# Half of the experts' second product turned round: weights stationary in 64-column tiles, the other half still streaming

## The reference, cut to what matters

```python
xe = xf[idx]                                                       # 16 x 80 x 1024
he = silu(einsum('ecd,edf->ecf', xe, w1)) * einsum('ecd,edf->ecf', xe, w3)
ye = einsum('ecf,efd->ecd', he, w2) * gate[..., None]              # w2: 1024 x 1024 for each expert
y = zeros_like(xf).at[idx.reshape(-1)].add(ye.reshape(-1, dm))
```

## Time and profile before

| | |
|---|---|
| time, median of 3 executions | 3217.52 us (3211.68 to 3217.69) |
| profiled execution | 3212.84 us, span 3211.0 us |
| TensorE clock granted, mean | 0.915 of full speed |
| PE busy | 2661.8 us (83%) |
| PEld busy | 1809.8 us (56%) |
| DVE, ACT, POOL busy | 1150.1, 464.4, 755.2 us |
| bytes moved by DMA | 552.70 MB |
| the two experts' stages | 1053 to 1601 us, 2633 to 3178 us |

### The profile page before, as it was taken

How to read it: one execution, slowest core, us unless ns; L and a number is a source line. 1 busy time by engine, 2 the same in 40 slices (tenths; PEclk the granted TensorE clock), 3 DMA queues, 4 the chain that set the end, 5 groups by cost and what they waited for, 6 DMA issues and landing times. The chain is left out here.

```text
span 3211.0 us, 72150 instructions
## 1 busy us (share of the span) xinstructions
PE 2661.8 (83%) x32434; PEld 1809.8 (56%) x32434; DVE 1150.1 (36%) x2476; ACT 464.4 (14%) x957; POOL 755.2 (24%) x886
## 2 busy tenths in 40 slices
PE   6998874778784899999879978566786849999995
PEld 3564554628643666766435645355385347676672
DVE  1002668775534111111130046786845241111112
ACT  1002331042111000000020033302311010000001
POOL 0002808435212000000010046272432220000002
PEclk9998996889986999999989999877998969999997
DMA  6101000050043899999731010001400549999994
GB/s 268 59 0 39 1 10 3 1 216 5 28 198 132 319 390 398 397 393 400 269 152 46 0 39 1 10 3 47 172 30 3 209 173 379 394 390 396 400 374 140
DMA packets 73210, 552.70 MB, mean 172 GB/s; under 512 B 13848, under 2 KB 15704, under 8 KB 33992
## 3 DMA queue, kind: packets, MB, share of 16 engines
q1 hardware_dynamic: 66760, 527.11, 41.3%
q0 software_dynamic: 6144, 20.98, 2.8%
HBM read 523.54 MB, written 24.51 MB: 171 GB/s over the span
## 5 line engine op out<-in xcount | busy, mean ns | idle before, releaser
L2352 PEld LDWEIGHTS ps<-arena 128*64 128x64 f32 x16384 | 579.8, 138 | 87.3 <-issue 84.7
L2352 PE MATMUL ps<-arena 128*64 128x80 f32 x16384 | 600.2, 234 | 11.7 <-issue 7.1
L2366 PE MATMUL ps<-arena 128*80 128x512 f32 x1024 | 466.7, 600 | 0.0
L517 PE MATMUL ps<-arena 128*128 128x128 f32 (+1 forms) x1088 | 296.4, 435 | 5.3 <-DVE arena L570 5.3
L2427 DVE TENSOR_TENSOR arena<-arena,ps 128x160 f32<-128x160 f32 x128 | 41.1, 321 | 719.8 <-ACT arena L2387 719.8
L2366 PEld LDWEIGHTS ps<-arena 128*80 128x80 f32 x1024 | 143.7, 149 | 229.8 <-issue 218.9
L517 PEld LDWEIGHTS ps<-arena 128*128 128x128 f32 x1088 | 164.9, 192 | 137.0 <-issue 131.2
L2387 ACT ACTIVATE arena<-ps 128x160 f32<-128x160 f32 x128 | 38.9, 304 | 1006.1 <-PE ps L2352 1006.1
L2113 POOL DMA_INDIRECT sum_d<-arena x32 | 45.6, 1426 | 583.6 <-DVE arena L2419 583.6
L574 DVE COPY arena<-ps 128x128 f32<-128x128 f32 (+3 forms) x48 | 16.3, 340 | 399.5 <-PE ps L517 287.6
L2107 POOL DMA_INDIRECT arena<-h_d,arena x32 | 40.2, 1256 | 497.2 <-DVEq L2402 430.0
(11 more groups left out here) (343 smaller groups left out, 3904.8 us busy)
## 6 DMA issues: line engine op xcount, KB each, us to landing
arena<-in_ex_w SPq DMA_DIRECT2D x128, 2048.0 KB, 16.1
arena<-in_ex_w SPq DMA_DIRECT2D x128, 1024.0 KB, 14.8
arena<-in_ada_w SPq DMA_DIRECT2D x32, 1024.0 KB, 8.0
arena<-in_w_t SPq DMA_DIRECT2D x34, 512.0 KB, 3.3
arena<-in_ada_w SPq DMA_DIRECT2D x8, 2048.0 KB, 17.2
arena<-in_w_tok SPq DMA_DIRECT2D x2, 3712.0 KB, 16.6
h_d<-x_sb SPq DMA_DIRECT2D x10, 512.0 KB, 2.6
sum_d<-x_sb SPq DMA_DIRECT2D x10, 512.0 KB, 13.7
```

What stands on the lines that cost most here:

```text
L517: i = nc.tensor.matmul(ps[:, n % 8, 0:c1 - c0], ring[:, a % WRING, k, :], e.hT[:, k, c0:c1], start=k == 0, stop=k == KD - 1)
L2352: m = nc.tensor.matmul(gated(j)[c * 64:(c + 1) * 64, f, a, :], w13[q % WG][:, a, k, f * P + c * 64:f * P + (c + 1) * 64], xT[:, x % 2, k, ...
L2366: m = nc.tensor.matmul(rows_out(x, h), he[:, x % 2, f, :], w2[:, q % WP, f % 2, h * 512:(h + 1) * 512], start=f == 0, stop=f == KD - 1)
```

## The change

`layout` packs `w2` in another way: half of its columns (0 to 511) in four blocks of 128 columns, each with all 1024 rows, the other half as before. A load is still 1 MB, 8 KB in each partition. In `project(x, j)` columns 512 to 1023 are made as before, with half the matmuls. Columns 128 j to 128 j + 127 are made with the weights stationary in 128 x 64 tiles and `he` streaming: 16 matmuls, whose result has columns in partitions. ScalarE copies those results from PSUM (`turned_columns`, once for each expert), TensorE transposes them back to rows (`turn_rows`, 4 transposes for each expert), and VectorE scales the rows as before, one quarter later than before. The stored sums now wait on `yr_ps` in place of `pr_ps`.

```diff
-        "ex_w2": f("ex_w2").reshape(DEPTH, NE, 4, 2, P, DM).transpose(0, 1, 2, 4, 3, 5),
     }
+    w2 = f("ex_w2").reshape(DEPTH, NE, KD, P, 2, 512)
+    still = w2[..., 0, :].reshape(DEPTH, NE, KD, P, 4, P).transpose(0, 1, 4, 3, 2, 5).reshape(DEPTH, NE, 4, P, 1024)
+    moving = w2[..., 1, :].reshape(DEPTH, NE, 4, 2, P, 512).transpose(0, 1, 2, 4, 3, 5).reshape(DEPTH, NE, 4, P, 1024)
+    out["ex_w2"] = np.concatenate([moving, still], 4)
...
-        return ps[0:CAP, 4 + 2 * (x % 2) + h, :]
+        return ps[0:CAP, 4 + 2 * (x % 2) if h else 7, :]
+
+    columns_out = ps[:, 5, 0:4 * CAP].rearrange("p (b n) -> p b n", b=4)
...
+                w = w2[:, q % WP, 0:1024].rearrange("p (f n) -> p f n", f=2)
                 for f in range(2 * j, 2 * j + 2):
-                    for h in range(2):
-                        m = nc.tensor.matmul(rows_out(x, h), he[:, x % 2, f, :], w2[:, q % WP, f % 2, h * 512:(h + 1) * 512],
-                                             start=f == 0, stop=f == KD - 1)
+                    nc.tensor.matmul(rows_out(x, 1), he[:, x % 2, f, :], w[:, f % 2, :], start=f == 0, stop=f == KD - 1)
+                if j == 0 and x:
+                    pe.wait_ge(S["yt_sb"], x)
+                w = w2[:, q % WP, 1024:].rearrange("p (f n) -> p f n", f=KD)
+                for f in range(KD):
+                    for c in range(2):
+                        m = nc.tensor.matmul(columns_out[c * 64:(c + 1) * 64, j, :], w[:, f, c * 64:(c + 1) * 64],
+                                             he[:, x % 2, f, :], start=f == 0, stop=f == KD - 1)
                 m.then_inc(S["pr_ps"], 1)
+
+            def turn_rows(x):
+
+                pe.wait_ge(S["yt_sb"], x + 1)
+                if x:
+                    pe.wait_ge(S["y_sb"], x)
+                for b in range(4):
+                    m = nc.tensor.transpose(rows_out(x, 0)[:, b * P:(b + 1) * P], yT[:, b, :], e.ident[:, :])
+                m.then_inc(S["yr_ps"], 1)
...
                     gate(x, j)
+                    if j == 0 and x >= 2:
+                        turn_rows(x - 2)
                     if x:
                         project(x - 1, j)
                     if j == 1 and x + 1 < NE:
                         turn_tokens(x + 1)
+            turn_rows(NE - 2)
             for j in range(4):
                 project(NE - 1, j)
+            turn_rows(NE - 1)
...
+            def turned_columns(x):
+
+                act.wait_ge(S["pr_ps"], 4 * x + 4)
+                if x:
+                    act.wait_ge(S["yr_ps"], x)
+                nc.scalar.activation(yT, columns_out, ACT.Copy).then_inc(S["yt_sb"], 1)
+
...
+                if q % 4 == 3 and q > 4:
+                    turned_columns(q // 4 - 1)
+            turned_columns(NE - 1)
...
-                dve.wait_ge(S["pr_ps"], 4 * x + 4)
+                dve.wait_ge(S["yr_ps"], x + 1)
...
+                    if j == 0 and x >= 2:
+                        weighed(x - 2)
                     if j == 1 and x + 1 < NE:
                         tokens(x + 1)
-                if x:
-                    weighed(x - 1)
+            weighed(NE - 2)
             weighed(NE - 1)
```

More of the change, by code:

```diff
@@ L2093, in expert_memory @@
     r["g2"], z = e.part(z, DM, rows=CAP)
+    r["yT"], z = e.part(z, 4, CAP)
     r["kept"] = z
@@ L2099, in expert_memory @@
     r["early"] = gate_place(0)
-    r["w2"] = e.part(first, WP, 2, DM)[0]
+    r["w2"] = e.part(first, WP, 2048)[0]
     r["w13"] = [e.part(gate_place(q), 2, KD, 256)[0] for q in range(WG)]
@@ L2128, in load_w2 @@
 def load_w2(e, sp, q, mem):
-    sp.dma_start(mem["w2"][:, q % WP].rearrange("p f n -> p (f n)"), e.d["ex_w2"][e.l, q // 4, q % 4].rearrange("p f n -> p (f n)")
+    sp.dma_start(mem["w2"][:, q % WP], e.d["ex_w2"][e.l, q // 4, q % 4]
                  ).then_inc(e.S[f"ld_f{q % WP}"], 16)
@@ L2261 @@
 EXPERTS_SEMS = (
-    "ld_g2r", "xe_used", "xt_ps", "xt_sb", "xm", "xa", "pr_ps", "y_sb", "ld_n2", "he", "hs", "h_ps",
+    "ld_g2r", "xe_used", "xt_ps", "xt_sb", "xm", "xa", "pr_ps", "yt_sb", "yr_ps", "y_sb", "ld_n2", "he", "hs", "h_ps",
 )
@@ L2271, in phase_experts @@
     mem = expert_memory(e)
-    w13, w2, xe, xT, hs, he, yR, g2, gv = (mem[k] for k in ("w13", "w2", "xe", "xT", "hs", "he", "yR", "g2", "gv"))
+    w13, w2, xe, xT, hs, he, yT, yR, g2, gv = (mem[k] for k in ("w13", "w2", "xe", "xT", "hs", "he", "yT", "yR", "g2", "gv"))
     NI = NE // 2
```

## The result

The changed kernel takes **3234.44 us** (median of 5 runs, 3223.87 to 3235.57) where the kernel before takes 3217.52 us (3211.68 to 3217.69): over all runs a ratio of 1.0049, with a 95% interval of 1.0035 to 1.0063 (the two medians alone give 1.0053). The forecast was 3192 us and faster, with a range of 3164 to 3228. The change makes the kernel slower, by 0.5%, and the time lies above the range. The profiled execution is the shortest of the five, and by itself inside the range: 3223.87 us, span 3221.9 us, 10.9 above the span before. What follows is about these 10.9 us.

What follows compares the result with a forecast made beforehand. TensorE was taken to pace the stage, with the DMA already slightly slower. Gains of 13.2 and 12.7 us less 2 x 0.4 make 25.1: 3212.84 becomes 3187.7, with 4.7 for the median 3192 us; range 3164 to 3228.

Steps and rivals of the forecast that it cites:

- TensorE's work: Experts' stage: a project takes 3.02 us instead of 3.59, 0.57 less; transposes add 0.63 an expert.
- The transposes: `turn_rows`, four 128 x 128 transposes for each expert: 0.156 us each, 0.63 us taken.
- The two hand-overs of 0.1: Around ScalarE's copy at the end of a stage: with the copy's 0.48, TensorE stands 0.7 us.
- TensorE alone: Rival, 13%: DMA delivers faster than 395 GB/s once asked sooner; TensorE decides, 24.4 us a layer gained, 3168.7 us.
- The fetches: Instruction stream of TensorE, one 16 KB fetch for 256 records: 52 fetches in 400 us become about 62.
- The DMA's part: Experts' stages: full DMA at 395 GB/s delivers nothing sooner and decides; 13.2 and 12.7 us gained in the two layers.
- the load of quarter 57: Last second-matrix load issued before `gate` weights run out: issued 1526.0, landed 1542.6; project(15, 0) then starts at 1557.8.
- the tail: End of a stage, from the start of project(15, 0) to VectorE's start: 17.8 us, 0.4 later than before.
- c: Time of one instruction fetch under a full DMA: just under 6.2 us taken, bounds 4.58 and 6.81.
- no gain: Start of project(15, 0) unchanged at c = 6.36 us; each further 0.1 us costs 7.7 us a layer.
- D: Rival, 17%: fetches at c above 6.4 make the kernel slower; c = 6.5 gives 3238 us, 6.81 gives 3286.
- case A: Experts' stages: the DMA's lag decides; 3192 us, own range 3180 to 3206, chance 50%.

Runs made afterwards that it cites:

- light loads: Only the w1 half of a gate's load fetched from quarter 6 on: changed kernel 3161.24 us, kernel before 3204.14 us.
- the quarter split: Changed kernel with 256 of the 1024 columns made with stationary weights and 768 streaming: 3252.05 us, ratio 1.0118.
- four pieces: Kernel before with every 512-column streaming pass of the second product cut into four of 128 columns: 3236.73 us.
- eight: Kernel before with every 512-column streaming pass cut into eight of 64 columns: 3370.51 us, with half of the gate's weights loaded 3347.46 us.

## Why the prediction was wrong

**TensorE's work: right but for one term.** The streaming half is 4 passes 0.43 apart, the stationary 32 take 1.16, a project is 3.0 us, the copy 0.44 (0.48 forecast). The transposes put 0.4 us into an expert, not 0.63, 3 us a stage less than forecast. The two hand-overs of 0.1 had no row; with them TensorE was to stand 0.7 us at the end of the stage, and it stands idle for 0.54. From project(14, 3) to VectorE's start it is 17.95 us in both layers (17.8 forecast). The copy is covered in mid-stage. With light loads TensorE alone gains what was worked out (25.4 and 27.1 us for 24.4).

**The fetches: counted right.** 62 for 52 in 400 us.

**The DMA's part: the rate right, the case not reached.** The engines stay at 1.01 and 389 to 395 GB/s, and the load of quarter 57, issued at 1525.9 us, lands after 14.7 us, at 1540.6, not after more than 25. 15.2 us behind that landing, at 1555.8, project(14, 3) could have started. It started at 1570.69, and PE waits for no weights: TensorE, not the loads, is 14.9 us late. TensorE, held back by its own instructions, never ran ahead of the loads, so the buffers had nothing to lend. Of the forecast's gain of 25.9 us before the tail (13.2 and 12.7) nothing is left.

**The step that failed:** "With one per c us, project(15, 0) starts at 1082.2 + 76.9 c", with c "just under 6.2". This puts the mean of TensorE's need, 6.05 us a block, against the time of a fetch. But each block waits for its own fetch. In the changed kernel with light loads, where nothing stalls, blocks last 4.4 to 6.9 us, mean 6.0: dense ones of gate passes alone, and long ones with streaming passes. A long block gets nothing for its length, and a dense one waits. In the changed kernel all 28 blocks whose own work is 4.4 to 4.5 us were stalled while the DMA was full (the first block of each stage apart), and nine tenths of the time lost at block ends stand behind blocks whose own work is under 6.15 us. Take for each of those 75 blocks in 450 us the longer of its own time and the 6.15 us that I chose: the mean is 6.36, "no gain" by the formula's own 6.36. With 6.35, the time of a typical stalled block in the changed kernel (medians 6.4 and 6.3), it is 6.44. Measured from the first project to project(14, 3): (1570.69 - 1079.14) / 76.9 = 6.39, and (3164.41 - 2668.96) / 76.9 = 6.44. The forecast had the right c within 0.2 us and the wrong sum.

Two smaller faults stand in the same paragraph. Its blocks count passes and weight loads alone. TensorE's waits for semaphores are records too, 145 in this stretch, so it has 77.5 blocks, of 6.34 and 6.40 us, and gains nothing from 6.32 on. And c is no floor ("a denser stream cannot run faster"): the 28 dense blocks lasted 5.0 to 7.0 us, medians 6.1 and 6.3.

**Which case it was: D, in a milder form.** The mechanism of D (17%) decided, stalls at block ends and no growing landing times, at 6.39 and 6.44 instead of "above 6.4". Two of its signs did not come: the DMA share stayed at 1.01, because the loads fill what TensorE's waiting leaves them, and the clock fell once. I had named the evidence, and the earlier trace rows, and gave the less weight to it because it came from the first 30 us of the stage. The chosen c made the fetches and the DMA's lag end at the same time, so the stated 3192 rested on case A alone.

The Trainium skill ("Runtime: NRT & Kernel Launch", Instruction fetch mechanics) says that these fetches are hidden behind the sequencer's issue. The run with light loads agrees (no stall at a share of 0.85), the changed kernel does not (51.9 us of "issue" at 1.01).

What stays open: how a fetch's time depends on what stands in the queues (median stalled blocks of 5.6 us at a share of 0.95, 6.3 to 6.4 at 1.01; unstalled ones of 4.7 at 0.97 and 354 GB/s; and an instruction packet that starts 3.6 us after its block in the changed kernel but 2.7 in the kernel before, both at 1.01), and why the runs of the changed kernel spread by 12 us.

## What to carry to other kernels

Where weights stream at the DMA's full rate, an instruction stream is a transfer too: divide TensorE's records, its semaphore waits among them, into blocks of 256 and compare the time of the densest blocks, not the mean, with the distance of resumes that the trace shows in such a stretch. A change that makes the work shorter by using more and smaller instructions can then buy waiting. This tells where stalls will stand, not their size: the longer of own time and 6.35 us, summed over 450 us, gives 31 us of stalls for the changed kernel (25 and 29 measured), but 18 for the quarter split (22 and 26), 18 for four pieces (10 and 6), 30 for eight (2 and 5) and 6 for the kernel before (none). Test it by lightening the loads in both kernels: what only the changed one gains is the fetch.

## What the runs showed of the hardware

- With the DMA full at 389 to 395 GB/s, blocks of 256 TensorE records whose own work is 4.4 to 4.5 us took 5.0 to 7.0 us (median 6.1 and 6.3 in the two layers of the changed kernel); at 289 GB/s (share 0.85) 4.4.
- For each block of 256 TensorE records (semaphore waits counted) the instruction queue moves one packet of 16 KB, about 1.0 us long. TensorE's stalls at block ends last until 1.2 to 1.6 us after its end. It starts 3.6 us after the preceding block end in the changed kernel, 1.5 to 1.7 with light loads.
- A pass with 80 columns through 128 x 128 weights costs 0.115 us, through one of a pair of 64-column tiles 0.036: the pair is 1.6 times as fast for the same weights.
- Streaming passes through 80 columns of weights: 512 columns 0.43 us, 128 columns 0.114, 64 columns 0.074.
- Semaphore increments on TensorE's queue follow each other by 0.15 us; 24 behind a matmul leave TensorE idle for 1.9 us (median), at a mean granted clock of 0.69.
